# Index products of the third and fourth tile of tokens: both column halves in one loop, bank by bank in turn

## What is computed

```python
for l in range(2):
    h = rms_norm(x, norm_g[l])
    proj = h @ w_in[l]                      # (512, 1024) @ (1024, 6728)
    a_u, a_v, a_z, b_q, b_k, b_v, b_z, i_q, i_k, i_w, g_a, g_b = split_columns(proj)
    y_a = spatial_gating(gelu(a_u), gelu(a_v), a_z)
    qi, ki = rope(i_q), rope(i_k)           # 8 heads of 64, one key of 64
    score = sum_h(i_w[:, h] * relu(qi[:, h] @ ki.T))   # 128 keys a query are kept
    y_b = attention(rope(norm(b_q)), rope(norm(b_k)), b_v, top128(score)) * silu(b_z)
    merged = sigmoid(g_a) * (y_a @ w_oa[l]) + sigmoid(g_b) * (y_b @ w_ob[l])
    x = x + merged @ w_out[l]
```

## Time and profile before

| | us |
|---|---|
| median of 3 runs | 799.05 |
| lowest and highest run | 795.96 and 800.09 |
| profiled execution, its own time | 797.74 |
| its span, first to last instruction | 795.9 |

### The profile page before, as it was taken

How to read it: one execution, slowest core, us unless ns; L and a number is a source line. 1 busy time by engine, 2 the same in 40 slices (tenths; PEclk the granted TensorE clock), 3 DMA queues, 4 the chain that set the end, 5 groups by cost and what they waited for, 6 DMA issues and landing times.

```text
span 795.9 us, 10742 instructions
## 1 busy us (share of the span) xinstructions
PE 785.0 (99%) x3836; PEld 661.0 (83%) x3836; DVE 587.5 (74%) x1026; ACT 353.5 (44%) x658; POOL 110.9 (14%) x101
## 2 busy tenths in 40 slices
PE   6999999999999999999999999999999999999998
PEld 6988888888888888888899888888888888888886
DVE  4859999978766673359986799999786658423895
ACT  5556645342344424333664775433334342335242
POOL 1137520000000000011211674000000000000130
PEclk9999999999999999999999999999999999999999
DMA  9625232323232222185873522323223222224574
GB/s 332 198 93 163 80 93 68 106 80 106 79 106 63 71 79 94 66 235 121 189 238 85 181 81 80 105 80 106 82 78 106 80 79 72 71 96 161 131 142 122
DMA packets 41572, 91.53 MB, mean 115 GB/s; under 512 B 2864, under 2 KB 3056, under 8 KB 41520
## 3 DMA queue, kind: packets, MB, share of 16 engines
q1 hardware_dynamic: 33408, 69.21, 27.7%
q0 software_dynamic: 7824, 21.06, 11.2%
q10 hardware_dynamic: 288, 0.59, 0.2%
HBM read 84.56 MB, written 6.29 MB: 114 GB/s over the span
## 4 chain that ended last, share of the span: by engine, by line
PE 94%; DVE 3%; DMA 2%; issue 0%; ACT 0%; SPq 0%; DVEq 0%; ACTq 0%
PE bank L702 23%; PE bank L700 23%; PE bank L701 23%; PE bank L784 5%; PE bank L734 3%; PE bank L736 3%; PE bank L735 3%; PE bank L674 2%; PE bank L692 2%; DMA x_sb<-in_x 2%; PE bank L630 1%; PE bank L683 1%; PE bank L645 1%; PE bank L644 1%; PE bank L615 1%; DVE w_lo L1149 1%
## 5 line engine op out<-in xcount | busy, mean ns | idle before, releaser
L700 PE MATMUL bank<-h_lo,w_hi 128*128 128x512 f32 x448 | 180.6, 403 | 0.0
L1149 DVE TENSOR_TENSOR w_lo<-w_raw,w_hi 128x1024 fp32r<-128x1024 f32 x132 | 172.2, 1319 | 10.0 <-ACT w_hi L867 6.8
L702 PE MATMUL bank<-h_hi,w_hi 128*128 128x512 f32 x448 | 174.7, 390 | 0.0
L701 PE MATMUL bank<-h_hi,w_lo 128*128 128x512 f32 x448 | 174.4, 389 | 0.0
L867 ACT ACTIVATE w_hi<-w_raw 128x1024 fp32r<-128x1024 f32 x132 | 135.6, 1055 | 22.1 <-DMA w_raw<-in_w_out 13.9
L700 PE MATMUL bank<-w_lo,h_hi 128*128 128x512 f32 x256 | 100.5, 393 | 0.0
L702 PE MATMUL bank<-w_hi,h_hi 128*128 128x512 f32 x256 | 99.9, 390 | 0.0
L701 PE MATMUL bank<-w_hi,h_lo 128*128 128x512 f32 x256 | 99.9, 390 | 0.0
L701 PEld LDWEIGHTS bank<-h_hi,w_lo 128*128 128x128 f32 x448 | 84.2, 188 | 18.6 <-issue 1.4
L700 PEld LDWEIGHTS bank<-h_lo,w_hi 128*128 128x128 f32 x448 | 84.2, 188 | 18.4 <-issue 1.4
L702 PEld LDWEIGHTS bank<-h_hi,w_hi 128*128 128x128 f32 x448 | 84.1, 188 | 17.9
(11 more groups left out here) (174 smaller groups left out, 1365.5 us busy)
## 6 DMA issues: line engine op xcount, KB each, us to landing
w_raw<-in_w_in SPq DMA_DIRECT2D x96, 512.0 KB, 3.8
w_raw<-in_w_out POOLq DMA_DIRECT2D x16, 512.0 KB, 6.2
w_raw<-in_w_out SPq DMA_DIRECT2D x12, 512.0 KB, 3.4
out<-x_sb POOLq DMA_DIRECT2D x4, 1024.0 KB, 5.8
w_raw<-in_w_oa SPq DMA_DIRECT2D x8, 512.0 KB, 3.4
w_raw<-in_w_ob SPq DMA_DIRECT2D x8, 512.0 KB, 3.4
x_sb<-out POOLq DMA_DIRECT2D x2, 2048.0 KB, 8.4
x_sb<-in_x SPq DMA_DIRECT2D x4, 512.0 KB, 9.1
```

Of the source, the lines that this page charges most:

```text
L700: nc.tensor.matmul(dst, s_h, m_l, start=(n == 0), stop=False)
L701: nc.tensor.matmul(dst, s_l, m_h, start=False, stop=False)
L702: last = nc.tensor.matmul(dst, s_h, m_h, start=False, stop=(n == len(pairs) - 1))
L1149: nc.vector.tensor_tensor(lo, w_raw[:, raw_slot(layer, u)], hi.bitcast(F32), ALU.subtract) \
```

## The change

For the third and fourth tile (t = 2 and 3) one loop over k from 0 to 9 takes the place of the two halves' loops. In it a product of step k into bank t % 3 is followed by a product of step k - 2 into bank 7, three such pairs a step; at k = 0 and 1 there are only the first, at k = 8 and 9 only the second. The wait for s_small stands ahead of step k = 2, so behind 6 products instead of 24. The waits for h_lo and the x transposes stay at k = 4, ahead of which there are now 18 products instead of 12. The five transposes of the rotated tile stand at k = 8, with 6 products behind them instead of 12. The first and second tile keep their order. The 48 products of a tile are the same ones as before.

```diff
+                pairs = (h_hi, index_lo), (h_lo, index_hi), (h_hi, index_hi)
+
+                def product(dst, first, k, n, width=half):
+                    h, w = pairs[n]
+                    return nc.tensor.matmul(dst[:, 0:width], h[:, k, tok], w[:, k, first:first + width],
+                                            start=(k == 0 and n == 0), stop=(k == KD - 1 and n == 2))
+
                 def products(dst, first, k, width=half):
-                    for n, (h, w) in enumerate(((h_hi, index_lo), (h_lo, index_hi), (h_hi, index_hi))):
-                        last = nc.tensor.matmul(dst[:, 0:width], h[:, k, tok], w[:, k, first:first + width],
-                                                start=(k == 0 and n == 0), stop=(k == KD - 1 and n == 2))
+                    for n in range(3):
+                        last = product(dst, first, k, n, width)
                     return last
...
-                for ks in ((range(KD // 2), range(KD // 2, KD)) if t == 0 else (range(KD),)):
+                if t >= 2:
+                    for k in range(KD + 2):
+                        if k in (0, KD // 2):
+                            pe.wait_ge(s_hlo.sem, s_hlo.at(layer, 2 * t + k // (KD // 2) + 1))
+                        if k == KD // 2 and t + 1 < TILES:
+                            transpose_x(layer, t + 1)
+                        if k == 2:
+                            pe.wait_ge(s_small.sem, s_small.at(layer, t))
+                        if t == 2 and k == KD:
+                            transpose_rotated(layer, 0)
+                        for pair in range(3):
+                            if k < KD:
+                                product(bank[t % GBANKS], 0, k, pair)
+                            if k >= 2:
+                                last = product(bank[7], half, k - 2, pair)
+                    last.then_inc(s_job.sem, 1)
+                    return
+
+                for ks in (range(KD // 2), range(KD // 2, KD)):
                     for k in ks:
...
                     pe.wait_ge(s_small.sem, s_small.at(layer, t))
                     for k in ks:
-                        if t == 2 and k == KD // 2:
-                            transpose_rotated(layer, 0)
                         last = products(bank[7], half, k)
```

## The result

The changed kernel takes 800.44 us (median of 20 runs, 798.62 to 806.85) against 798.31 us for the kernel before (20 runs, 795.96 to 801.30): a ratio of 1.0036 with a 95% interval of 1.0022 to 1.0051. That is 2.9 us slower by the ratio and 2.1 by the medians, clear of noise, and within the 0.5% that the prediction calls the same. The profiled execution has a span of 800.0 us; lines after the edit stand 22 further down (L784 is L786 by its place, since the matmul moved into `product`; L923 is L945, L924 is L946, L920 is L942, L989 is L1011, L991 is L1013).

A forecast was written before the change was run, and what follows sets the result against it. TensorE's own work bounds the kernel (94% of 795.9 us). A new fourth-tile stall, less the third tile's gain, gives +1.21 us a layer, +2.4 in all: 800.2 or 801.5 by starting value, so 800.8; range 797.5 to 804.0.

The forecast's parts named there:

- The zero for the whole alternation: Index products of third and fourth tile: alternating banks neither gains nor costs time, as the one bank change seen shows.
- loss bound of 6 ns: Alternating products, 144 in all: at most 6 ns lost each, 0.9 us, from rounding of the one step seen.
- Step (a) and (c): Third tile: TensorE's 0.27 us stall ahead of the x transposes (a) is hidden behind six bank 7 products (c).
- Step (b): Third tile, wait for ScalarE's copy ahead of the seventh product: stall 0.05 us, and a fill of 0.08 once more.
- Steps (d) to (f): Rest of third tile: eight transposes 0.82, 24 products and step into rotated transposes 3.39, last of those five 0.46 us later.
- The lower bound: Sum over both layers at least +2.0 us, taking 0.11 instead of 0.26 us from an engine's end to TensorE's start.
- the two starting values: Times before the change: profiled execution 797.74 us and median of the three runs 799.05 us.
- Rival 1: Index products: alternation removes the whole 12.3 ns rest of each step; +0.6 us in all, 799.1; chance 0.12.
- Rival 2: Fourth tile's new 1.26 us stall lowers the clock, 1.4 us a layer; +5.2 us, 806 us; chance 0.05.
- the first kernel's two stretches: First layer before the change: half clock after TensorE stood 2.97 us, full clock around a stall of 0.86.
- Rival 3: Fourth tile: ScalarE's copies arrive in time, leaving only the third tile's gain; -0.3 us, 798.1; chance 0.05.
- rival 4: After the fourth tile: a later wait swallows part of the delay; +1.2 us, 799.6; chance 0.05.

## Why the prediction was right

- **The bound.** TensorE's queue carried every change to the end. From the transpose behind the fourth tile of the second layer to the end of the span it is 795.9 - 431.14 = 364.76 us before and 800.0 - 435.18 = 364.82 after, and 364.7 to 364.9 in every other profiled execution.
- **Products.** That the bank makes no difference was right, and the reading of the one step from bank 0 to bank 7 with it. The zero for the whole alternation was off by 1.6 to 1.9 ns a step, 0.06 us a tile, inside the loss bound of 6 ns. It is the price of the operands' order, which I hadn't thought of and which a view in steps of 10 ns couldn't have shown.
- **Step (a) and (c), the old stall.** 0.27 us, gone as said.
- **Step (b), the wait ahead of the seventh product.** I had 0.05 us of stall, from 0.26 us between ScalarE's end and the reader's start. Behind the stage copies it was 0.16 to TensorE (429.22 to 429.38). The 0.26 was GpSimd's row, behind one semaphore addition more and on another engine; no stall appeared here, only the fill.
- **Steps (d) to (f).** 0.79, 3.32 and 0.43 us for 0.82, 3.39 and 0.46: the terms had come from rows in which TensorE had just stood. In the 3.39 the step into the rotated transposes was 0.21 us, 422.30 to 422.51, behind the low half of h that ended at 422.36, so it held a short wait that the new order no longer has. With (b) they make the third tile 8.05 us instead of the 8.22 that I had.
- **The fourth tile.** 2.00 us from the last transpose to the stage copy, 0.72 for the copies: both exact. With 0.16 for 0.26 the wait ends at 2.88 instead of 2.98. The excess is 1.16 instead of 1.26. That the fourth tile still came out at 7.75 for 7.77 is two errors that cancel: the 42 products behind the wait took 5.80 us (429.38 to 435.18) where I had 5.71.
- **Sum.** +1.02 a layer instead of +1.21, +2.0 instead of +2.4 us, 0.17 of the difference from the third tile. The lower bound said +2.0 as well, but partly by luck: it shortened both stalls with a latency of 0.11 us, where 0.16 was measured, and it had neither the shorter (d) to (f) nor the dearer products behind the wait. A latency read at TensorE should have been taken all the same; GpSimd's was a row of another reader.
- **The time.** 800.44 against 800.8, and +2.1 (medians) or +2.9 us (ratio) against +2.4. That the median hits to 0.4 us is luck, as the runs of one kernel spread over 5 us and more. The range's lower end, 797.5, doesn't follow from its own terms: +0.2 us on the two starting values gives 798.6, and 2 us of scatter 796.6; nothing hangs on it. The queue accounts for +2.0 and the clock can account for the rest: seven of the 20 runs had a mean granted clock of 0.989 to 0.994 and took 801.75 to 806.85 us, while the eleven at 0.998 or more have a median of 799.75. The kernel before, in the 74 executions timed beside the experiments, was that low in 14, and its 43 at 0.998 or more have medians of 797.5 to 797.7 in each set. At equal clock the difference is thus 2.1 to 2.2 us, a rough figure, as it compares executions of different sets. Whether the change makes the low clock more frequent, these counts don't tell.
- **Rival 1** (the bank hides 12 ns) fell: 6.43 us with the banks in turn. **Rival 2** (the clock) did not come with this stall in the profiled execution: granted clock 1.00 and steps of 134 to 135 ns in the second layer's fourth tile, and in the first layer's too. Its mechanism exists and showed at 2.60 us, at 1.5 us a layer, close to the price that it was given (1.4). That only a long idle lowers the clock, as I read from the first kernel's two stretches, doesn't hold: the changed kernel's start-up lost it behind 0.44 us. **Rival 3** (copies in time) fell with the new row of 1.0 us, **rival 4** (a later wait swallows it) with the 364.8 us that remain behind.

The Trainium skill, "TensorE: Matmul & The Clock Gate", section "Back-to-back issue gap", gives N/2.4 + 2.5 ns for an isolated matmul at full clock, by my estimate 124.2 ns for 292 columns. The trace doesn't agree: no order tried here came below 133 ns on average.

## What to carry to other kernels

When a step moves along a queue that bounds the kernel, list every chain that starts from it on other engines and measure its length from its start to the waiter's release; the new stall is that length less the work that still stands between. Moving a wait from behind 24 products to behind 6 costs nothing where the producer's chain still fits (the third tile) and what is left of the chain where it doesn't (0.48 us in the fourth tile even with the transposes left in their place); the best cure here was a buffer that needs no wait (fourth tile 6.49 us), next the order of the producer's own queue (6.88). One step in the old trace at which a condition changes, such as the bank, can settle what a rewrite with 144 such steps would bring, but only for that condition: ask what else alternates with it.

## What the runs showed that I had not expected

The order in which matmuls read their operands has a small price at full clock: with operands alternating between steps k and k - 2 and between two column ranges, 48 products took 6.49 us, in the old order 6.43, in groups of three 6.40, while the bank written made no difference. And a stall's length alone doesn't tell whether TensorE keeps its clock: in profiled executions 1.80 us of idle kept it four times and 2.37 once, 2.60 lost it twice, and in one start-up it went behind no more than 0.44.
